# Second feed-forward projection as seven products in four parts, with operand sums on GpSimd and seven planes per chunk pair in DRAM

## The reference, cut to what matters

```python
def swiglu(xn, p):
    return (jax.nn.silu(xn @ p['ffn_w_gate']) * (xn @ p['ffn_w_up'])) @ p['ffn_w_down']

f = swiglu(rmsnorm(x, p['norm_ffn_pre']), p)
x = x + rmsnorm(f, p['norm_ffn_post'])
```

## Time and profile before

| | us |
|---|---|
| median of three runs | 3089.73 |
| span of the profiled execution | 3087.5 |
| PE busy | 3016.0 (98%) |
| DVE busy | 1862.8 (60%) |
| ACT busy | 1258.0 (41%) |
| GpSimd (POOL) busy | 175.8 (6%) |
| first to last matmul start of the down stage | 2556.4 to 3063.1 |
| time after the last down matmul, within the span | 24 |

### The profile page before, as it was taken

One profiled execution on the slowest core, in us unless ns is written; L12 is line 12 of the kernel. 1 busy time (PEld: TensorE's weight loads), 2 busy tenths in 40 slices (PEclk: granted clock), 3 DMA queues, 4 the chain that ended last, 5 costly groups with the idle time before them and its releaser, 6 DMA issues.

```text
span 3087.5 us, 59894 instructions
## 1 busy us (share of the span) xinstructions
PE 3016.0 (98%) x24137; PEld 2902.2 (94%) x24137; DVE 1862.8 (60%) x2689; ACT 1258.0 (41%) x1939; POOL 175.8 (6%) x220
## 2 busy tenths in 40 slices
PE   8999999999999999999997999999999999999999
PEld 6789999998879999987796999999999999999999
DVE  4544336454765477666368888888888884322323
ACT  5442444334365565334355434344334343321323
POOL 0000000001253000010000000000000001000010
PEclk9999999999999999999999999999999999999999
DMA  7553223332216567886664433333433344432323
GB/s 272 186 181 109 83 77 88 95 89 79 70 42 213 157 192 250 282 327 213 249 209 141 127 120 119 116 116 113 121 119 119 116 124 155 143 97 95 103 92 142
DMA packets 454969, 442.98 MB, mean 143 GB/s; under 512 B 22251, under 2 KB 417804, under 8 KB 446943
## 3 DMA queue, kind: packets, MB, share of 16 engines
q1 hardware_dynamic: 436634, 360.81, 38.0%
q0 software_dynamic: 12416, 69.55, 6.2%
q10 hardware_dynamic: 5776, 10.62, 1.0%
HBM read 407.22 MB, written 33.95 MB: 143 GB/s over the span
## 4 chain that ended last, share of the span: by engine, by line
PE 88%; DVE 6%; ACT 3%; DMA 2%; issue 1%; POOL 0%; ACTq 0%; DVEq 0%; SPq 0%; POOLq 0%
PE ps L3069 16%; PE ps L3707 16%; PE ps L3478 16%; PE ps L3673 9%; PE ps L3675 9%; PE ps L3674 9%; PE ps L3066 5%; DVE w_low L1958 1%; ACT w_high L1171 1%; DMA w_raw<-in_xa_wo 1%; PE ps L3569 1%; DMA q_wide<-q_mid 1%; PE ps L3733 0%; PE ps L3297 0%; PE ps L3108 0%
## 5 line engine op out<-in xcount | busy, mean ns | idle before, releaser
L1958 DVE TENSOR_TENSOR w_low<-w_raw,w_high 128x1024 fp32r<-128x1024 f32 x354 | 435.0, 1229 | 620.8 <-ACT w_high L1171 620.1
L3673 PE MATMUL ps<-set_high,w_hi 128*128 128x260 f32 x2352 | 664.9, 283 | 2.7 <-ACT prods L1806 1.5
L3675 PE MATMUL ps<-set_high,w_lo 128*128 128x260 f32 x2352 | 665.5, 283 | 0.0
L3674 PE MATMUL ps<-set_low,w_hi 128*128 128x260 f32 x2352 | 665.4, 283 | 0.0
L1171 ACT ACTIVATE w_high<-w_raw 128x1024 fp32r<-128x1024 f32 x356 | 377.1, 1060 | 640.7 <-PE ps L3478 301.4
L3673 PEld LDWEIGHTS ps<-set_high,w_hi 128*128 128x128 f32 x2352 | 443.6, 189 | 3.1 <-issue 1.7
L3675 PEld LDWEIGHTS ps<-set_high,w_lo 128*128 128x128 f32 x2352 | 444.6, 189 | 0.0
L3674 PEld LDWEIGHTS ps<-set_low,w_hi 128*128 128x128 f32 x2352 | 443.2, 188 | 0.0
L1735 ACT ACTIVATE w_hi<-raw 128x768 fp32r<-128x768 f32 x168 | 142.3, 847 | 469.6 <-PE ps L3675 469.6
L3069 PE MATMUL ps<-x_high,w_high 128*128 128x260 f32 x1568 | 318.8, 285 | 2.1 <-DVE w_low L1958 2.0
L3069 PE MATMUL ps<-x_low,w_high 128*128 128x260 f32 x1568 | 314.4, 282 | 0.0
(11 more groups left out here) (546 smaller groups left out, 5638.3 us busy)
## 6 DMA issues: line engine op xcount, KB each, us to landing
w_raw<-in_w_in SPq DMA_DIRECT2D x96, 512.0 KB
raw<-in_ffn_w_up SPq DMA_DIRECT2D x176, 256.0 KB, 2.9
raw<-in_ffn_w_gate SPq DMA_DIRECT2D x176, 256.0 KB, 3.2
raw<-in_ffn_w_down SPq DMA_DIRECT2D x176, 256.0 KB, 3.1
w_raw<-in_w_out SPq DMA_DIRECT2D x64, 512.0 KB
w_raw<-in_xa_wq SPq DMA_DIRECT2D x64, 512.0 KB
w_raw<-in_xa_wo SPq DMA_DIRECT2D x64, 512.0 KB
w_raw<-in_xa_wk SPq DMA_DIRECT2D x32, 512.0 KB
```

Of the source, the lines that this page charges most:

```text
L1958: dve.tensor_tensor(w_low[:, slot], w_raw[:, (g.slab0 + jj) % RAW], w_high[:, slot].bitcast(F32), ALU.subtract).then_inc(sem("w_low_ready" ...
L3673: pe.matmul(ps[:, bank, 0:HALF], high, set_high[:, kp, x], start=kp == 0, stop=False)
L3674: pe.matmul(ps[:, bank, 0:HALF], high, set_low[:, kp, x], start=False, stop=False)
L3675: ins = pe.matmul(ps[:, bank, 0:HALF], low, set_high[:, kp, x], start=False, stop=kp == KP - 1)
```

## The change

The down product goes by the same seven-product scheme, with 2x2 blocks out of a pair of output chunks, pairs of hidden chunks and the two token halves. A slab takes 7 x 2 x 3 = 42 matmuls instead of 48. There are four parts (12, 12, 12 and 8 chunks; units of 3, 3, 3 and 2 slabs), and still 88 slabs.

- Planes of the hidden chunks: a pair of chunks becomes seven planes of 260 columns. SP stores the three that are blocks of h_out, GpSimd computes four sums (`hidden_sums`, L992 on in its place, four operations of 260 columns per pair) and stores them in two DMAs. h_mid grows from 4 to 7 planes of 260 per pair.
- ACT's queue loads a whole pair (7 x 260 columns, 910 KB) into `set_raw`, which is the place of set_low (`set_load`); ACT makes set_high of it in one copy of 1820 columns, DVE set_low in one subtraction of 1820 columns. There are 22 pairs; the set holds eight. `hidden` waits also for the sums of the pair before.
- Weight sums of the down slabs: three GpSimd operations per slab (512, 256, 256 columns; `down_sum`), allowed when the low part of the slab two before it is made. ACT and DVE then do two operations each per slab (768 columns of blocks, 1024 of sums) where they did one of 1024.
- Outputs: `first_product` (ACT) and `combine` (DVE) after every unit as in the up stage; then ACT copies (part 0), GpSimd adds (`add_out`, parts 1 and 2), or DVE adds (part 3). The squares' sum stays on GpSimd. All seven banks belong to a unit, so units no longer alternate between two halves of PSUM.
- The last unit has its own order of additions (`last_out`), and x_last comes in three pieces.

The core of the diff, GpSimd first, then ACT (from `down_high` on), then DVE's loop (the last hunk):

```diff
-            for c in range(FF):
-                pool.wait_ge(sem(f"h_stored{c % 2}"), 16 * (c // 2 + 1))
...
-                pool.dma_start(h_in[h_from(c)][:], h_mid[:, c * T:(c + 1) * T]).then_inc(sem(f"h_loaded{h_from(c)}"), 16)
+            def hidden_sums(j):
+                pool.wait_ge(sem("h_made"), j * 2 + 2)
...
+                pool.tensor_tensor(h_sums[:, 1], h_out[0][:, HALF:T], h_out[1][:, HALF:T], ALU.add).then_inc(sem("h_sums"), 1)
+                pool.tensor_tensor(h_sums[:, 0], h_out[0][:, HALF:T], h_out[0][:, 0:HALF], ALU.subtract).then_inc(sem("h_sums"), 1)
...
+            def down_sum(n):
+                raw_, t = raw[n % 4], sums_of(n)
+                pool.wait_ge(sem(f"raw_loaded{n % 4}"), 32 * (n // 4 + 1))
+                pool.wait_ge(sem("w_low"), max(n - 1, UP))
...
+                pool.tensor_tensor(t[:, 0:2].rearrange("p s a c -> p a s c"), raw_[:, :, 0:1].to_broadcast([P, 2, 2, P]), raw_[:, :, 1:3],
+                                   ALU.subtract).then_inc(sem("down_summed"), 1)
+                pool.wait_ge(sem("down_summed"), done + 1)
+                pool.tensor_tensor(t[:, 2], raw_[:, :, 1], t[:, 1], ALU.subtract).then_inc(sem("down_summed"), 1)
+                pool.wait_ge(sem("down_summed"), done + 2)
+                pool.tensor_tensor(t[:, 3], raw_[:, :, 3], t[:, 2], ALU.subtract).then_inc(sem("down_summed"), 1)
...
+            down_sum(UP)
+            down_sum(UP + 1)
+            hidden_sums(HP - 1)
+            for w, (p, v, n0, ns) in enumerate(UNITS):
+                for n in range(n0, n0 + ns):
+                    if n + 2 < END:
+                        down_sum(n + 2)
+                    if n == n0 and w:
+                        if UNITS[w - 1][0] in (1, 2):
+                            add_out(w - 1)
+                        elif UNITS[w - 1][0] == 3:
+                            for c in (2 * v - 2, 2 * v - 1):
+                                add_square(c)
...
+            def down_high(n):
+                act.wait_ge(sem("w_used"), n - (3 if n < UP + 2 else 1))
...
+                act.wait_ge(sem("down_summed"), 3 * (n - UP) + 3)
+                act.activation(w_hi[k][:, 6:14], sums_of(n)[:].rearrange("p s a c -> p (s a) c"), ACT.Copy).then_inc(sem("w_high"), 1)
...
+            down_high(UP)
+            set_load(0)
+            set_load(1)
+            down_high(UP + 1)
+            set_load(2)
+            set_load(3)
+            set_high_down(0)
+            set_high_down(1)
+            set_load(4)
+            set_load(5)
+            set_high_down(2)
+            set_high_down(3)
             first_product(FF - 1)
+            set_high_down(4)
+            set_high_down(5)
             gated(FF - 1)
...
             for w, (p, v, n0, ns) in enumerate(UNITS):
+                for n in range(n0, n0 + ns):
+                    if UP + 2 <= n + 1 < END:
+                        down_high(n + 1)
+                    for kp in range(6, HP):
+                        if set_load_at(kp) == n + 1:
+                            set_load(kp)
+                    for kp in SET_AT.get(n + 1, ()):
+                        set_high_down(kp)
+                    if n == n0 and w and UNITS[w - 1][0] == 0:
+                        copy_out(w - 1)
...
+                first_product(FF + w)
...
+            for w, (p, v, n0, ns) in enumerate(UNITS):
+                for n in range(n0, n0 + ns):
+                    if UP + 2 <= n + 1 < END:
+                        down_low(n + 1)
+                    for kp in SET_AT.get(n + 1, ()):
+                        set_low_down(kp)
+                if w < len(UNITS) - 1:
+                    down_out(w)
```

More of the change, by code:

```diff
@@ L324, in build @@
         h_out = [at(f"h_out{k}", [P, T], F32, H_OUT + k * TB) for k in range(2)]
[L325 removed]
+        h_sums = at("h_sums", [P, 4, HALF], F32, H_OUT + 2 * TB)
         SET = max(arena0, H_OUT + 4 * TB)
@@ L509, in weight @@
             return tile[:, 6 + 2 * ("S3", "S1", "S2", "S4").index(name) + kp]
-        PARTS = [(0, 8), (8, 20), (28, 16)]
-        assert sum(n for _, n in PARTS) == FF and 28 == HS and all(n % KS == 0 for _, n in PARTS)
+        PARTS = [(0, 12), (12, 12), (24, 12), (36, 8)]
+        assert sum(n for _, n in PARTS) == FF and all(n % KS == 0 for _, n in PARTS)
         UNITS = []
@@ L565, in build, with set_load_at, sums_of, ffn_chunk @@
+        def set_load_at(kp):
+            return max(slot_free(kp) + 1, UP + 1)
+        SET_AT = {}
+        for kp in range(6, HP):
+            SET_AT.setdefault(set_load_at(kp) + 1, []).append(kp)
+        assert all(n + 1 <= used_at(kp) for n, kps in SET_AT.items() for kp in kps)
+        def sums_of(n):
+            return (w_sums if type(n) is not int or n < UP + 2 else down_sums)[n % 2]
+        def ffn_chunk(c):
+            return c ^ 1
         params = ([(0, NORM[n], NC, i[n][0]) for n in norm_names]
@@ L1888, in _ @@
+            act.activation(y_spare[:], eps_col[:], ACT.Sqrt)
+            y_x_copied(0)
+            square_out(len(UNITS) - 1)
             for a in (1, 2):
@@ L3744, in _ @@
                 rows = P if t < TT else B
-                ins = pe.matmul(ps[0:rows, Y_SUMS, t:t + 1], ssum[:, t * P:t * P + rows], ones[:, 0:1], start=True, stop=True)
+                ins = pe.matmul(ps[0:rows, Y_SUMS, t:t + 1], out_ssum[:, t * P:t * P + rows], ones[:, 0:1], start=True, stop=True)
             ins.then_inc(sem("out_summed"), 1)
```

344 lines of the change are left out of this document (172 added, 172 removed).

## The result

The changed kernel takes 3107.39 us (median of four runs, 3106.68 to 3109.38) beside 3089.14 us for the kernel before: ratio 1.0062, 95% interval 1.0049 to 1.0074. It is 18 us slower where 9.5 us less were forecast: outside the forecast's own range (3062 to 3100), just inside the wide one (3044 to 3108), and in the other direction. The profiled execution has a span of 3107.8 us and took 3109.38.

What follows compares the result with a forecast made beforehand. The down stage was taken as bound by its number of matmuls, 4224 x 0.1199 = 506.3 us. Terms -63.3 + 15.8 (start) + 22 + 6 + 10 = -9.5 gave 3089.7 - 9.5 = 3080.2 us; own range 3062 to 3100, wide 3044 to 3108.

Steps and rivals of the forecast that it cites:

- matmuls: Down stage: 88 slabs with 6 matmuls fewer each, 528 at 0.1199 us, 63.3 us less on PE.
- start: Start of the down stage: three PE waits in turn, 3.9, 8.8 and 3.9, sum 16.6 us; bounds 8 and 18.
- boundaries: Set loads where parts change: exclusive time 9 us over at each of the first two, 4 at the third; 22 us.
- output sums in parts 1 and 2: GpSimd's add_out delays a low part in one unit of two, PE waits 1.1 to 1.2; 6 us, bounds 0 and 19.
- part 3: Last part: 2.0 us over in six units, less the 2 us GpSimd is ahead; 10 us, bounds 0 and 14.
- tail, up stage: Kernel's end and the up stage: both stay as they were, costed at 0.
- The mechanism: Down stage: DVE and GpSimd operations with both inputs in SBUF exclude each other, 4.27 of 5.03 us held per slab.
- The first rival: Exclusion harmless, DVE and GpSimd fit in each other's gaps: 43.1 us less, 3046.6; chance 0.18.
- The second: Rival: exclusion lasts each whole operation and bounds the kernel from part 1 on, units of 17.2 us; +40, 3130; chance 0.20.
- lead of 2 us: Part 3: GpSimd is ahead by 2 us, which was subtracted from that part's waits.
- Clock: Long PE waits may lower PE's clock: some 1.5 us, for waits of 9 us once, inside the bounds.
- Late sets (third rival): Set loads of 910 KB run at 250 GB/s, second of each pair 1 to 2 us later: +8, 3088; chance 0.12.

Runs made afterwards that it cites:

- e1_add_dve: Against the changed kernel, the output sums of parts 1 and 2 run on DVE instead of GpSimd: 3088.94 us, ratio 1.0007.
- e2_sums_fill: Against the changed kernel, GpSimd's three weight sums per down slab became three fills that read nothing, leaving these sums out of the product: 3067.27 us, ratio 0.9934.
- e9_out_first: Against e8_all, DVE's combine goes ahead of the set splits at the end of each unit: 3077.57 us, ratio 0.9958.
- e3_pe_filled: Against the changed kernel, PE issues matmuls into an unread bank where it was known to wait 3 us or more: 3106.18 us, ratio 1.0059.
- e4_late_hidden: Against the changed kernel, GpSimd's sums of the last hidden pair go behind its sums for the stage's fourth slab: 3105.88 us, ratio 1.0056.
- e10_all_filled: Against e8_all, PE issues matmuls into an unused bank at its six waits of about 3 us: 3073.94 us, ratio 0.9949.
- e8_all: Against the changed kernel, the edits of e1_add_dve and of e5 to e7 together: 3075.57 us, ratio 0.9957.
- e5 to e7: Three single edits, each against e1_add_dve: last hidden pair's sums spread over slabs (0.9983), six set splits moved to mid-part (0.9988), sums of squares on DVE (0.9985).

## Why the prediction was wrong, step by step

The forecast's terms against what was measured. The output sums' term is the difference between the change and e1_add_dve; the boundaries, the start and part 3 are taken without them.

| term | forecast | measured | from |
|---|---|---|---|
| matmuls | -63.3 | -63.3 | 3696 for 4224, at 0.1199 |
| start | 16.6 | 19.7 | e1_add_dve |
| boundaries | 22 | 29.5 | e1_add_dve: 10.9 + 12.9 + 5.7 |
| steady units of parts 1 and 2 | 0 | 2.0 | e1_add_dve |
| output sums in parts 1 and 2 | 6 | 17.5 | 82.4 - 64.9 |
| part 3 | 10 | 13.8 | both kernels |
| sum of the excess | 54.6 | 82.5 | |

27.9 us more; with the forecast's -9.5 that is +18.4, and 18.2 were measured. That the two agree to 0.2 us is luck: the table is of one execution, and the two profiled spans, 3087.5 and 3107.8, differ by 20.3, of which 2.0 arise ahead of the stage.

- **Matmuls, tail, up stage: right.** The time behind the last down matmul is 24 us as before. In the up stage GpSimd's four operations hold DVE now and then, but from 1712 us to the stage's end PE has no wait in either kernel. The changed kernel's stage begins 2.0 us later than the other's. That is no cost of the change: the up stage's first matmul is already 3.1 us later, and in the changed kernel and its twelve variants, which are alike up to there, the stage begins anywhere from 2552.6 to 2561.2.
- **The mechanism: right.** e2_sums_fill shows it: without the reads of GpSimd's weight sums 38 of the 82 us go. PE's waits sum to 61.1 us, where about 55 were forecast, and POOL is busy 711 us, where over 250 were. The first rival (no exclusion, 3046.6) is out. The second had the rule, but its full price (units of 17.2 us) is not what happened either: they took 16.4. Even so 3107 is nearer to its 3130 than to my 3080. Its point of decision, "0.1 us more than I take at about 100 places", was passed.
- **Output sums: the step that failed.** "In one unit of two" came from working through a queue in which the meeting of `add_out` and the low part varies. It doesn't vary: the wait that it causes shifts ACT, DVE and GpSimd alike, and the two meet again in every unit. All 16 units have it, at 1.0 to 1.1 us in each of the ten steady ones, and 6.8 us at the boundaries: 17.5, where I had half as many and took 6. The price of one meeting was right (1.1 to 1.2), and my upper bound of 19 is what nearly came. No row supported that "part of the waits are absorbed", and little was.
- **Boundaries: mis-sized**, 29.5 for 22 (10.9, 12.9 and 5.7 for 9, 9 and 4; the second is beyond its bound of 12). I asked how much exclusive time was wanted and found 9 us over, but DVE also has work that excludes nobody: `combine` at 2.5 us in each unit. By the means of e1_add_dve, DVE has over slabs 22 to 27 some 6 x (1.25 + 1.62) + 6 x 2.45 + 2 x 2.5 + 1.4 = 38.3 us of work for 30.2, which is 8 over. DVE without a pause there (e9_out_first) shows that it sets the pace; but neither count alone gives 10.9 or 12.9, and that the two limits together make the difference is argued, not shown.
- **Start: two of three waits right, short in its sum.** The waits were forecast as 3.9, 8.8 and 3.9 and came out as 3.7, 7.2 and 0.6, with 0.7 more at the second product. By PE's starts the waits sum to 13.8 us, less than my 16.6, and 5.0 us are matmuls at the lower clock behind the first and the 7.2, so the excess is larger. e3_pe_filled shows that these two are one account: with the clock up, the start's excess is 20.7. No run removes the first wait alone, so my remark that whoever does finds the second is untested; e4_late_hidden, which removes the second, found others behind it.
- **Part 3: mis-sized**, 13.8 for 10. Six intervals between units, as many as forecast, ran 11.8 to 12.8 us for 10.07 (mean 12.3, forecast 12.0), and a seventh 0.4 over: 13.8. Of the lead of 2 us that I subtracted nothing is seen. Boundary 3 lies just ahead, with its own excess; that it used the lead up is argued, not shown.
- **Clock: seen wrongly, at little cost.** 21 us at 1.2 GHz instead of 1.5, but e3_pe_filled and e10_all_filled gain at most 1 to 2 us when most of it is taken away. Where DVE sets the pace, slow matmuls use time that PE would have waited. Adding them to the waits as a separate term would have been an error; the excess contains both.
- **Late sets (third rival):** a load of 910 KB lands 6.9 us after its issue in the median, between the 4 and the 7 that I reckoned for two in a row. The sign that I named is not there: in slabs 23 and 47 ACT has no idle time before set_high. In slab 24 a load ends 0.28 and 0.78 us of it and in slab 48 0.18, but DVE is busy with other work meanwhile and begins each of these low parts without a pause. At the start loads end 3.9 us of ACT's idle time in five waits, ahead of PE's first wait of 3.7; that wait was in the forecast.

The step that made most of the miss is the output sums' term, 11.5 of the 27.9 us; the boundaries follow with 7.5. The direction was missed because a gain of 63 us stood against a price of 55 made of terms that all draw on the same two engines, so that they err together: each came out higher, by 2 to 12 us, where the margin was 9.5.

What stays open: the split of the 50 us that e8_all still has. e2_sums_fill has 44 with the output sums still in it, so part is exclusion by the weight sums, but both edits together were not run. Open too is why boundary 2 costs 2 us more than boundary 1. For e5 to e7 the ratios give 2 to 4 us more than the table; the two come from different executions, and the table's one execution per kernel can't settle that. Nor are the ratios that sure: each is good to 0.001 (3 us), and e1_add_dve was measured in another series than e5 to e7.

## What to carry to other kernels

Work given to GpSimd beside a busy DVE can cost DVE up to its own duration where both read two operands from SBUF (2.2 us on a low part beside an output sum of 2.4); count both engines' reads as one queue, and DVE's whole work as a second limit. In a loop where two engines meet, ask whether a wait preserves the meeting: here it did in all 16 units. Of moves between the two, the longest uninterrupted GpSimd operation was the best to take back to DVE (16 additions: 17 us), and a block in front of a deadline was better cut up than moved (7 us against 2).
